# Sixteen of 256 expert dots through TensorE, a dense V part of 960 columns, and V rows gathered later

## The reference

```python
def chunk(xc):                       # 128 tokens
    ...
    best_s, best_pos = lax.top_k(cand_s, PEER_TOPK)
    expert_idx = jnp.take_along_axis(cand_i, best_pos, axis=-1)
    g = jax.nn.softmax(best_s, axis=-1)
    u = expert_u[expert_idx]
    vv = expert_v[expert_idx]
    act = jax.nn.gelu(jnp.einsum('chkd,cd->chk', u, xc, preferred_element_type=jnp.float32))
    return jnp.einsum('chk,chkd->cd', (g * act).astype(vv.dtype), vv)
```

## Time and profile before

| | us |
|---|---|
| median of 3 runs | 1690.18 |
| lowest, highest | 1689.35, 1695.68 |
| the profiled execution's own time | 1694.34 |
| its span, first to last instruction | 1692.5 |
| first dot starts, last dot ends | 463.3, 1200.8 |
| first and last dense product | 1280.0, 1666.4 |
| busy: TensorE, VectorE, ScalarE, GpSimd | 1234.9, 1298.5, 460.9, 842.8 |
| moved from and to memory | 575 MB, 340 GB/s over the span |

### The profile page before, as it was taken

The page is one execution under the profiler, slowest core; times in us unless marked ns, Lnnn a source line. Parts: engine busy times, 40 slices in busy tenths (PEclk is TensorE's granted clock), DMA queues, the critical chain, the costliest instruction groups (busy, mean ns, idle before and its releaser), DMA issues.

```text
span 1692.5 us, 14464 instructions
## 1 busy us (share of the span) xinstructions
PE 1234.9 (73%) x4812; PEld 839.8 (50%) x4812; DVE 1298.5 (77%) x1802; ACT 460.9 (27%) x1023; POOL 842.8 (50%) x546
## 2 busy tenths in 40 slices
PE   9999999999995554001344544454699999999993
PEld 7888887778984343000122322332365555555551
DVE  5554666466699999999999999999796665666667
ACT  5333443554200100000135565552381000000000
POOL 1000010000174888877888888888565443444444
PEclk9999999999997778555666676666699999999997
DMA  8886546348799999999999999999899999999998
GB/s 237 223 207 196 169 143 213 99 148 278 260 410 415 422 411 396 385 371 362 395 382 407 403 413 387 398 401 422 335 313 380 410 409 411 410 410 409 410 409 347
DMA packets 150230, 575.81 MB, mean 340 GB/s; under 512 B 15586, under 2 KB 28596, under 8 KB 117268
## 3 DMA queue, kind: packets, MB, share of 16 engines
q0 software_dynamic: 74384, 421.30, 62.6%
q1 hardware_dynamic: 75460, 152.82, 26.9%
q10 hardware_dynamic: 320, 0.86, 0.1%
HBM read 572.57 MB, written 2.36 MB: 340 GB/s over the span
## 4 chain that ended last, share of the span: by engine, by line
PE 30%; DVE 28%; DMA 24%; POOL 12%; issue 4%; ACT 2%; DVEq 0%; ACTq 0%; POOLq 0%
DMA v_rows<-in_peer_expert_v,pick_row 21%; DVE big L1549 10%; DVE more_rows L1549 8%; PE ps L1692 6%; PE ps L1694 6%; PE ps L1693 6%; POOL big L691 5%; PE ps L2095 4%; POOL more_rows L691 3%; DVE big L1597 3%; POOL v_rows L671 3%; DMA more_rows<-in_peer_expert_u,pick_row 2%; PE ps L2118 1%; DMA big<-in_peer_expert_u,pick_row 1%; DVE big L1574 1%
## 5 line engine op out<-in xcount | busy, mean ns | idle before, releaser
L671 POOL DMA_INDIRECT v_rows<-in_peer_expert_v,pick_row x256 | 307.8, 1202 | 271.7 <-DVE big L1597 234.9
L1597 DVE SCALAR_TENSOR_TENSOR big<-v_rows,pick_w,big 128x1152 f32<-128x1152 f32 x203 | 287.6, 1417 | 151.7 <-DMA v_rows<-in_peer_expert_v,pick_row 149.7
L2095 PE MATMUL ps<-v_rows,diag 128*128 128x512 f32 (+1 forms) x312 | 182.9, 746 | 269.5 <-DMA v_rows<-in_peer_expert_v,pick_row 169.8
L1549 DVE CUSTOM_DVE_ANT_0 big<-big 128x2048 f32<-128x2048 f32 x150 | 340.1, 2283 | 12.9 <-DMA big<-in_peer_expert_u,pick_row 12.5
L691 POOL DMA_INDIRECT big<-in_peer_expert_u,pick_row x150 | 288.8, 1925 | 65.6 <-issue 43.2
L2095 PEld LDWEIGHTS ps<-v_rows,diag 128*128 128x128 f32 x312 | 83.3, 285 | 368.2 <-issue 194.8
L691 POOL DMA_INDIRECT more_rows<-in_peer_expert_u,pick_row x106 | 222.7, 2101 | 75.3 <-issue 28.3
L1030 DVE TENSOR_TENSOR split_lo<-raw,split_hi 128x1024 fp32r<-128x1024 f32 x119 | 145.8, 1225 | 143.7 <-ACT split_hi L719 118.1
L1549 DVE CUSTOM_DVE_ANT_0 more_rows<-more_rows,big 128x2048 f32<-128x2048 f32 x106 | 240.8, 2284 | 11.0 <-DMA more_rows<-in_peer_expert_u,pick_row 11.0
L2127 PE MATMUL ps<-big,dense 128*128 128x512 f32 (+1 forms) x512 | 213.5, 539 | 0.3 <-DMA big<-in_peer_expert_v 0.3
L2127 PE MATMUL ps<-big 128*128 128x512 f32 (+1 forms) x512 | 213.4, 539 | 0.0
(11 more groups left out here) (281 smaller groups left out, 1495.2 us busy)
## 6 DMA issues: line engine op xcount, KB each, us to landing
big<-in_peer_expert_v SPq DMA_DIRECT2D x128, 448.0 KB, 6.8
raw<-in_w_in SPq DMA_DIRECT2D x88, 512.0 KB, 3.7
raw<-in_w_out SPq DMA_DIRECT2D x32, 512.0 KB, 5.1
big<-in_peer_w_query SPq DMA_DIRECT2D x16, 512.0 KB, 6.5
raw<-in_peer_w_query SPq DMA_DIRECT2D x8, 512.0 KB, 7.6
spare<-in_peer_w_query SPq DMA_DIRECT2D x8, 512.0 KB, 8.3
v_rows<-in_peer_expert_v,pick_row POOLq DMA_INDIRECT x256, 14.2
big<-in_peer_expert_u,pick_row POOLq DMA_INDIRECT x150, 9.1
```

The lines of the kernel that those rows point to most:

```text
L671: pool.indirect_dma_start(v_row(k), None, v_table, bass.IndirectOffsetOnAxis(pick_row[:, k:k + 1], 0)).then_inc(v_gathered[v_place(k)], 16)
L1549: dve.tensor_tensor_reduce(row, row, XN[:, place_of(m // TOPK)[0], :], 1.0, 0.0, ALU.mult, ALU.add, pick_dot[:, m:m + 1]).then_inc(dotted, 1)
L1597: dve.scalar_tensor_tensor(out=v, in0=row, scalar=pick_w[:, k:k + 1], in1=v, op0=ALU.mult, op1=ALU.add).then_inc(added, 1)
L2095: ins = pe.matmul(psf[:, c:c + w], diag[:, j % DIAGS, :], row[:, c:c + w], start=k == 0, stop=j == pe_adds(PICKS) - 1)
```

## The change

Three things change.

1. Picks 4 and 10 of heads 1 to 8, 16 in all (`TURNED_DOTS`), are no longer computed by VectorE over 128x2048. TensorE turns the pick's U rows block by block (16 transposes into two PSUM banks, four blocks to a bank), ScalarE copies each four blocks to SBUF (`turned_copies`, into the room of `diag`), and TensorE multiplies them with `x1t`, the turned x1, into a 128x128 result (`turned_dot`). Its diagonal holds the 128 dots; VectorE takes it with a product with the identity (`take_dot`), four picks later in its queue. The gather that follows in such a pick's place waits for the transposes and not for a dot.
2. V_ROW goes from 1152 to 1088, and the dense part from 896 to 960 columns.
3. V rows are gathered beside U rows after every third pick, first after pick 146, and there are 37 of them (`V_FROM`, `V_BESIDE`); all eight places serve U rows up to pick 138. In the seam VectorE adds a row beside every group from 1 on, 31 rows for 21. With TensorE's 16 as before, 84 rows are then added or under way before the dense stage for 73, and 172 stay for VectorE beside it.

```diff
-U_WIDE = 108
+U_WIDE = 138
-V_ROW = 1152
+V_ROW = 1088
-V_FROM, V_BESIDE = 112, 36
+V_FROM, V_BESIDE = 144, 37
-SEAM = sorted([(i, "dve", i) for i in range(GROUPS) if i % 3] + [(i + 2, "pe", i) for i in range(GROUPS) if i % 2])
+SEAM = sorted([(i, "dve", i) for i in range(1, GROUPS)] + [(i + 2, "pe", i) for i in range(GROUPS) if i % 2])
+TURNED_DOTS = [n * TOPK + k for n in range(1, NH + 1) for k in (4, 10)]
+TAKEN_AFTER = 4
+DOT_GROUPS = 4
+DOT_ORDER = [f for m in range(PICKS) for f in ([m] if m not in TURNED_DOTS else []) + ([m - TAKEN_AFTER] if m - TAKEN_AFTER in TURNED_DOTS else [])]
 def v_until(m):
-    return max(0, m - V_FROM + 1) // 4
+    return max(0, m - V_FROM + 1) // 3
...
                 f = before_in_place(m)
-                if f >= 0:
-                    pool.wait_ge(dotted, f + 1)
+                if f in TURNED_DOTS:
+                    pool.wait_ge(row_turned, DOT_GROUPS * (TURNED_DOTS.index(f) + 1))
+                elif f >= 0:
+                    pool.wait_ge(dotted, dots_until(f))
...
+            def turned_copies(q):
+                for g in range(q * DOT_GROUPS, (q + 1) * DOT_GROUPS):
+                    act.wait_ge(row_turned, g + 1)
+                    if g:
+                        act.wait_ge(turned_used, g)
+                    act.activation(turned_rows.rearrange("p c n -> p (c n)"), ps[:, g % 2, :], ACT.Copy).then_inc(turned_here, 1)
...
+            def take_dot(m):
+                q = TURNED_DOTS.index(m)
+                dve.wait_ge(turned_used, DOT_GROUPS * (q + 1))
+                dots = ps[:, 2 + q % 2, 0:P]
+                dve.tensor_tensor_reduce(dots, dots, ident[:, :], 1.0, 0.0, ALU.mult, ALU.add, pick_dot[:, m:m + 1]).then_inc(dotted, 1)
...
             for m in range(PICKS):
-                pick_dot_of(m)
+                if m not in TURNED_DOTS:
+                    pick_dot_of(m)
+                if m - TAKEN_AFTER in TURNED_DOTS:
+                    take_dot(m - TAKEN_AFTER)
...
+            def turned_dot(m):
+                q, t = TURNED_DOTS.index(m), place_of(m // TOPK)[0]
+                row = row_here(pe, m)
+                def turn(c):
+                    g = q * DOT_GROUPS + c
+                    if g >= 2:
+                        pe.wait_ge(turned_here, g - 1)
+                    for j in range(KC // DOT_GROUPS):
+                        k = c * DOT_GROUPS + j
+                        ins = pe.transpose(ps[:, g % 2, j * P:(j + 1) * P], row[:, k * P:(k + 1) * P], ident[:, :])
+                    ins.then_inc(row_turned, 1)
+                def add(c):
+                    if c == 0 and q >= 2:
+                        pe.wait_ge(dotted, dots_until(TURNED_DOTS[q - 2]))
+                    pe.wait_ge(turned_here, q * DOT_GROUPS + c + 1)
+                    for j in range(KC // DOT_GROUPS):
+                        k = c * DOT_GROUPS + j
+                        ins = pe.matmul(ps[:, 2 + q % 2, 0:P], turned_rows[:, j, :], x1t[:, k, t * P:(t + 1) * P], start=k == 0, stop=k == KC - 1)
+                    ins.then_inc(turned_used, 1)
+                turn(0)
+                for c in range(1, DOT_GROUPS):
+                    turn(c)
+                    add(c - 1)
+                add(DOT_GROUPS - 1)
```

More of the change, by code:

```diff
@@ L171, in uses_of_place, with dots_until @@
     return sum(u_place(f) == u_place(m) for f in range(m + 1))
+TURNED_DOTS = [n * TOPK + k for n in range(1, NH + 1) for k in (4, 10)]
+TAKEN_AFTER = 4
+DOT_GROUPS = 4
+DOT_ORDER = [f for m in range(PICKS) for f in ([m] if m not in TURNED_DOTS else []) + ([m - TAKEN_AFTER] if m - TAKEN_AFTER in TURNED_DOTS else [])]
+assert sorted(DOT_ORDER) == list(range(PICKS))
+DOT_PLACE = {f: i for i, f in enumerate(DOT_ORDER)}
+def dots_until(m):
+    return DOT_PLACE[m] + 1
 def v_place(k):
@@ L414, in layer @@
         query_used = sem("query_used")
+        row_turned, turned_here, turned_used = sem("row_turned"), sem("turned_here"), sem("turned_used")
+        turned_rows = diag[:, :, :]
+        ALL_TURNED = DOT_GROUPS * len(TURNED_DOTS)
         def query_name(n):
@@ L910, in pick_diag @@
             def pick_diag(m):
+                if m == 0:
+                    act.wait_ge(turned_used, ALL_TURNED)
                 if m % TOPK == 0 or m >= V_BESIDE:
@@ L960, in group_out @@
                 act.wait_ge(token_made, t * P + (i + 1) * GROUP_TOKENS)
+                if t == 0 and i == 0:
+                    act.wait_ge(turned_used, ALL_TURNED)
                 act.activation(dense_w[t][:, :, i * GROUP_TOKENS:(i + 1) * GROUP_TOKENS],
-                               ps[:, 3 + i % 2, :].rearrange("p (j a) -> p a j", j=GROUP_TOKENS), ACT.Copy).then_inc(group_moved, 1)
+                               ps[:, 4 - i % 2, :].rearrange("p (j a) -> p a j", j=GROUP_TOKENS), ACT.Copy).then_inc(group_moved, 1)
+            def turned_copies(q):
[4 more added lines that the diff above has]
+                    act.activation(turned_rows.rearrange("p c n -> p (c n)"), ps[:, g % 2, :], ACT.Copy).then_inc(turned_here, 1)
             for m in range(PICKS):
@@ L973, in _ @@
                     head_gelu(n - 1)
+                if m in TURNED_DOTS:
+                    turned_copies(TURNED_DOTS.index(m))
                 if m == TURN_0 + 1:
@@ L1625, in _ @@
             after()
-            dve.tensor_tensor(pick_exp[:, 0:TOPK], head_best, head_best[:, 0:1].broadcast_to([P, TOPK]), ALU.subtract).then_inc(sem("first_exp"), 1)
+            step(dve.tensor_tensor(pick_exp[:, 0:TOPK], head_best, head_best[:, 0:1].broadcast_to([P, TOPK]), ALU.subtract))
             first_rows(1, TOPK)
-            dve.wait_ge(sem("first_exp"), 1)
+            after()
             dve.wait_ge(sem("first_rows"), 2)
@@ L2089, in pick_add @@
                 if k == 0:
-                    pe.wait_ge(sem("pq_first"), 3)
+                    pe.wait_ge(dotted, dots_until(TURNED_DOTS[-1]))
                 j = pe_adds(k)
@@ L2096, in pick_add @@
                 ins.then_inc(pe_added, 1)
+            def turned_dot(m):
+                q, t = TURNED_DOTS.index(m), place_of(m // TOPK)[0]
+                row = row_here(pe, m)
+                if q == 0:
+                    pe.wait_ge(sem("pq_first"), 3)
+                def turn(c):
[19 more added lines that the diff above has]
+                add(DOT_GROUPS - 1)
             def turn_picks(t, parts):
@@ L2106, in group @@
             def group(t, i):
+                if t == 0 and i == 1:
+                    pe.wait_ge(dotted, dots_until(TURNED_DOTS[-1]))
                 if t * GROUPS + i >= 2:
@@ L2117, in group @@
                     hot = hot1[:, i % SEAM_HOT, :, j, :] if t else hot0[:, :, j, :]
-                    pe.matmul(ps[:, 3 + i % 2, j * P:(j + 1) * P], hot[:, 1, :], hot[:, 0, :], start=True, stop=True).then_inc(token_made, 1)
+                    pe.matmul(ps[:, 4 - i % 2, j * P:(j + 1) * P], hot[:, 1, :], hot[:, 0, :], start=True, stop=True).then_inc(token_made, 1)
             def dense(a):
@@ L2169, in _ @@
                     group(0, i)
+                if m in TURNED_DOTS:
+                    turned_dot(m)
                 if m == TURN_1:
```

6 lines of the change are left out of this document (2 added, 4 removed).

## The result

The changed kernel takes 1712.86 us (median of four executions, 1708.50 to 1717.35), the kernel before beside it 1690.36. The ratio is 1.0132, with a 95% interval from 1.0111 to 1.0153: slower by 1.3%, where 1696.5 was forecast.

The account below looks back on a forecast made before the run. Bounds: DMA, VectorE or GpSimd's full queue by heads in the picks, VectorE in the seam, TensorE in the dense stage. Picks -9.7, seam +9.3, dense +27.5, end -20.8 sum to +6.3: 1696.5 us, own range 1690 to 1702.

Parts of the forecast that it names:

- V rows later and denser: Heads 9 to 14: 32 V rows for 24 cost +14 us, between 9 by bytes and 19 by GpSimd issues.
- Heads 1 to 8: Pick stage: two dots a head off VectorE and V rows leaving heads 7 and 8 gain 26.7 us.
- Rival 2: Heads 1 to 4: TensorE becomes late, VectorE waits at PSUM sums, some 5 us a head; total 1716, chance 0.10.
- Rival 1: Pick stage: every extra gather costs a whole slot of GpSimd's full queue; total +16.5, 1706 us, chance 0.20.
- Seam: Tile 1's weights: 30 VectorE row adds for 20, less two falling into a 6.09 us stall, +9.3 us.
- GpSimd's wait for TensorE's last early row: Seam's start: met one gather sooner, but that row is also added sooner; 0 us, bounds -2 and +6.
- head 15: Last head of the pick stage: one V row more, +2 us.
- Dense stage: Dense V sum: TensorE's columns grow by 1920/1792, +27.5 us, with the DMA needing less time than TensorE.
- end: After TensorE's last product: V rows no longer end last, 26.1 us become 5.3, -20.8 us.
- heads 9 to 14 near 50 us with GpSimd on issue gaps alone: Confirming sign for the pick stage: about 50 us a head, GpSimd waiting only for its own issue gaps.
- VectorE's wait on TensorE: Refuting sign: VectorE waiting over 10 us in total on TensorE at the PSUM sums.
- Heads 3 to 6, the dense stage and TensorE's end: Confirming signs: 40 to 41 us a head, DMA share 1.0; dense stage 414 us; TensorE ending within 6 us of span's end.

Follow-up runs that it names:

- e2: Changed kernel with its early V rows gathered one pick sooner (V_FROM 143 for 144), nothing else changed: 1691.76 us.
- e8: Changed kernel with ScalarE making a V row's diagonal ahead of the group's moves and one-hot matrices of the same pick: 1694.95 us.
- e11: Changed kernel with TensorE leaving out columns 512 to 1023 of V rows 1 to 36 (output incomplete, timing only): 1694.31 us.
- e5: Changed kernel with a V row after every fourth pick instead of every third, 28 early rows for 37: 1681.16 us.
- e1: Changed kernel with V_ROW back at 1152, so the dense part is 896 columns wide: ratio 0.9997 to the kernel before.

## Why the prediction was wrong

**The step that failed** is "V rows later and denser ... I take +14, between the price in bytes and that in issues" (28.8 measured, 14.8 over; the other rows of the table give 7 of that back, which leaves +14.1 for +6.3). It priced the rows' gathers and stopped there. A V row is also a diagonal on ScalarE and 4 us on TensorE, and the prediction placed neither in its queue. The thing to look for was what TensorE is queued behind: `pick_add` waits for `pick_diag`, that for the weights of a group, and the next group of TensorE for `pick_add`. The trace of before had the turn in it, in a view that the prediction did not use. This is the chain of the kernel before from 890 to 1110 us:

```profile
by line: DVE big L1549 30.0%; DVE more_rows L1549 15.0%; PE ps L2095 11.4%; DVE big L1574 5.0%; POOL big L691 4.6%; DMA big<-in_peer_expert_u,pick_row 4.0%; PE ps L2118 3.9%; ACT big L948 3.3%; issue 2.4%; POOL v_rows L671 2.2%; ACT big L94
```

TensorE's adds are in the chain of before with 11%. From 880 to 1140 us, the stretch of the earlier trace rows, TensorE waited 15 times for a diagonal:

```profile
PE ps L2095 <- ACT diag L917: 91.2, 15, 8.9
```

These are twelve picks of it on TensorE, four groups (L2118) and three adds (L2095):

```profile
910.25 4.18 PE L2095 MATMUL ps<-v_rows,diag 128*128 128x512 f32 x6 [6.60 <-ACT diag L917]
914.22 1.87 PE L2118 MATMUL ps<-big 128*128 128x128 f32 x8
...
920.86 4.18 PE L2095 MATMUL ps<-v_rows,diag 128*128 128x512 f32 x6 [4.32 <-ACT diag L917]
924.83 1.70 PE L2118 MATMUL ps<-big 128*128 128x128 f32 x8
931.00 2.04 PE L2118 MATMUL ps<-big 128*128 128x128 f32 x8 [4.47 <-ACT big L948]
932.84 3.87 PE L2095 MATMUL ps<-v_rows,diag 128*128 128x512 f32 x6
937.79 1.13 PE L2118 MATMUL ps<-big 128*128 128x128 f32 x8 [1.08 <-ACT big L948]
```

Two rows in three waited for a diagonal and held up the group behind them; the turn between them is 10.6 us. The two turns without such an add take 6.5 and 5.9 us from group to group, so four turns need some 34 us (an estimate from these rows), and twelve picks of before last 36. At every third pick all four turns hold an add, 40 us, and there is no slack. The earlier trace rows was read as "GpSimd's queue is full", and so all attention went to GpSimd; the chain gives VectorE's dots 45% and the two lines of GpSimd that it shows 7%.

With the turn broken (e2) the kernel takes 1691.76 us, inside the forecast's own range, and heads 9 to 14 are at +8.2 against before (e8 +10.2, e11 +11.8): near the price in bytes, 9, and under the middle of 9 and 19.

**Heads 1 to 8**: right in kind and nearly in size, -29.9 for -26.7. A PSUM sum takes 0.294 us, for 0.33 estimated with its read, and heads 3 to 6 stand on the DMA, so the difference does not matter. This is the group of the sums, of after:

```profile
L1587 DVE CUSTOM_DVE_ANT_0 ps<-ps,ident 128x128 f32<-128x128 f32 x16 | 4.7, 294 | 0.0
```

**Rival 2** (TensorE late) fell with the same row: idle time before the sums is 0.0. The granted clock was 0.80 in heads 3 to 6 for 0.62 before, since the new work fills TensorE's gaps. The turned dot from 568.24 to 577.81 us took 9.6 us with the waits for ScalarE inside, under the 13 at which it would have mattered. GpSimd waited 7.4 us on the transposes over all eight heads.

**Rival 1** (a whole slot for each gather) came nearest, +16.5 for +22.5 of the medians and +14.1 of the spans, but for the wrong reason: that is luck. The extra gathers cost 1.4 us (e5 against e2), and 16 dots fewer did not keep heads 3 to 6 from the DMA's floor. The prediction also misread a row behind it. It took the issue of 0.94 us in the earlier trace rows for one without a dot beside it, and a dot began 0.07 us after it:

```profile
706.55 0.94 POOL L691 DMA_INDIRECT big<-in_peer_expert_u,pick_row  x1 [0.30 <-issue]
706.62 2.28 DVE L1549 CUSTOM_DVE_ANT_0 more_rows<-more_rows,big 128x2048 f32<-128x2048 f32 x1
```

What counts is which of the two starts first. In heads 3 to 6 of before all 58 gathers that started while a dot was running ended 0.81 to 0.83 us after that dot's end, and the six that started between dots took 0.93 to 1.04. The Trainium skill ("SBUF — State Buffer", Who interferes with whom) states the contention of a VectorE instruction with two SBUF inputs only for a GpSimd instruction that reads SBUF; a gather takes its row numbers from there, and these rows agree. Even so an extra gather did not cost a whole slot, as the price of 1.4 us says. No run shows whether the sums from PSUM leave GpSimd free.

**Seam**: +5.8 for +9.3. The adds cost what was said; the stall of 6.09 us for TensorE's late V row did not come, and one of 3.0 us for VectorE's own first row did. The prediction had put GpSimd's wait for TensorE's last early row at 0 (bounds -2 and +6); it was 10.2 us long, and VectorE waited 3.6 us in all for rows in the seam. For **head 15** it wrote 1.4 MB where the row's 1.4 us are meant; +2 stood for the 3.3 measured. **Dense stage** and **end**: right to 0.1 us. But the prediction never set the two against each other. With 172 rows and 896 columns little hangs over (9.4 us), so 27.5 and -20.8 was not the choice there was; e1 shows 22 us for it.

**The signs**: of those named, "heads 9 to 14 near 50 us with GpSimd on issue gaps alone" fell in after and holds in e2. VectorE's wait on TensorE was looked for at the PSUM sums alone, and came at L1611 and L1470. Heads 3 to 6, the dense stage and TensorE's end are as named; the seam is 3 us under its 88.

**Open**: 8 of the 22.5 us are not in the profiled pair, and why the executions of after spread over 9 us was not looked into. With the turn broken, GpSimd's queue and the DMA engines are both full in heads 9 to 14, and no run tells them apart.

## What to carry to other kernels

When work is moved to other places of a hand-written order, write down for each engine what it is queued behind, and look for a cycle in which two engines wait for each other once a period; its length, over the number of steps in it, is a bound that no busy share shows, and two periods that coincide (three and three) can cost what a shift by one step gives back. The direction of the shift matters: by the order of the queues a V row one pick later would still stand ahead of the group (not run, but the rows of before that fall there do wait for their diagonal). Take the chain of waits for the stretch that the change touches before settling on a bound, not the waits of one engine (e11 kept the long waits and lost the bound). And when two edits remove the same overhang, as fewer rows and narrower rows did here, price them against each other: the second one only leaves its cost.

## What the runs showed of the hardware

Heads 3 to 6 of after sustained 421 GB/s of gathered 8 KB rows with DMA share 1.01, 40.1 us for 16.8 MB; with V rows of 4.4 KB among them, heads 9 to 14 of e2 sustained 401 at a share of 1.00.

A gather's issue that starts during a dot of two SBUF inputs ended 0.81 to 0.83 us after the dot (58 of 58); one that starts ahead of it took 0.94 us and the dot ran beside it in its usual 2.28.

In the stretches where TensorE was busy about half of the time with pauses of some 5 us (heads 9 to 14, 27.3 of 53.5 us), it was granted 0.64 to 0.68, nearer the lower of its two levels, and an add of a V row took 4.07 us; in the seam of before, granted 0.90, an add of 1152 columns took 2.18 us (at 1269.72). That made the longest link of the turn as long as it was. The Trainium skill ("TensorE: Matmul & The Clock Gate", HAM oscillation) says that idle gaps throw the clock back to half, and the rows agree.
